# An eleven-place ring of expert weights kept up to expert 5, weight splits ordered behind the evictions, and two chunks of expert 1 requested during the last projection

## The reference

```python
h = layer_norm(x, ln0_g, ln0_b)
# mixer: proj = h @ w_in, cut into qkv, a, bt, z, xc, gb, gc, qm, gl (three gates)
qkv = silu(causal_depthwise_conv(qkv, conv_qkv)); q, k = l2_normalize(q), l2_normalize(k)
g = -(exp(a_log) * softplus(a + dt_bias)); beta = sigmoid(bt)
y_a = gated_rmsnorm(gated_delta_rule_chunked(q, k, v, g, beta)) * silu(z)
y_b = gb * causal_depthwise_conv(gc * xc, conv_mix)
y_m = softmax(qm @ km.T * 128 ** -0.5) @ vm          # km, vm = mem @ w_mem_kv
merged = sum(sigmoid(gl[b]) * (y[b] @ w_br[b]) for b in range(3))
h = layer_norm(ALPHA * h + merged @ w_o, ln1_g, ln1_b)
# experts: top 4 of 32 by h @ w_router + b_router, softmax over the four
for each expert e, for its tokens:
    gate, up = split(h @ w_gate_up[e] + b_gate_up[e])     # 1024 -> 2 x 1024
    hid = (clip(up, -7, 7) + 1) * (min(gate, 7) * sigmoid(1.702 * min(gate, 7)))
    ffn += weight * (hid @ w_down[e] + b_down[e])         # 1024 -> 1024
out = layer_norm(ALPHA * h + ffn, ln2_g, ln2_b)
```

## Times and profile before

| | us |
| --- | --- |
| median of 3 runs | 1283.3 |
| lowest, highest | 1281.4, 1283.37 |
| the profiled execution | 1282.62 |
| its span, first to last instruction | 1280.9 |
| TensorE busy in the span | 1217.3 (95%) |
| DMA moved | 453.62 MB, mean 354 GB/s |

### The profile page before, as it was taken

One profiled execution on the slowest core, in us unless ns is written; L12 is line 12 of the kernel. 1 busy time (PEld: TensorE's weight loads), 2 busy tenths in 40 slices (PEclk: granted clock), 3 DMA queues, 4 the chain that ended last, 5 costly groups with the idle time before them and its releaser, 6 DMA issues.

```text
span 1280.9 us, 16880 instructions
## 1 busy us (share of the span) xinstructions
PE 1217.3 (95%) x7135; PEld 616.2 (48%) x7135; DVE 392.6 (31%) x784; ACT 241.3 (19%) x387; POOL 146.1 (11%) x106
## 2 busy tenths in 40 slices
PE   6989999999999999999999999999999999999996
PEld 5789999998843333333333333333333333333332
DVE  5375553434521221221221221221112222122224
ACT  4355345444310000000000000000000000000001
POOL 8223432455200000000000000000000000000000
PEclk9899999999999999999999999999999999999998
DMA  9533323475799999999999999999999999999994
GB/s 299 200 133 132 115 85 128 171 304 196 277 401 420 398 427 426 420 431 428 430 435 428 431 430 427 433 431 427 430 430 430 432 432 426 429 432 430 426 425 179
DMA packets 49512, 453.62 MB, mean 354 GB/s; under 512 B 6110, under 2 KB 10283, under 8 KB 31019
## 3 DMA queue, kind: packets, MB, share of 16 engines
q1 hardware_dynamic: 49450, 452.71, 85.2%
HBM read 451.64 MB, written 1.05 MB: 353 GB/s over the span
## 4 chain that ended last, share of the span: by engine, by line
PE 72%; DMA 19%; DVE 3%; ACT 2%; POOL 2%; issue 1%; SPq 0%; ACTq 0%; DVEq 0%; POOLq 0%
PE bank L1386 27%; DMA late<-in_w_gate_up_dram 19%; PE bank L1459 13%; PE bank L1203 6%; PE bank L1204 5%; PE bank L1205 5%; PE bank L1472 4%; PE bank L1357 3%; PE bank L1372 2%; PE bank L1447 1%; ACT late L1175 1%; POOL w_lo L758 1%; ACT w_hi L1079 1%; PE bank L1467 1%; PE bank L559 1%
## 5 line engine op out<-in xcount | busy, mean ns | idle before, releaser
L1386 PE MATMUL bank<-late 128*64 128x512 f32 x1632 | 368.1, 598 | 10.4 <-DMA late<-in_w_gate_up_dram 10.2
L1386 PEld LDWEIGHTS bank<-late 128*64 128x64 f32 x1632 | 112.6, 137 | 242.2 <-issue 217.6
L1459 PE MATMUL bank<-late 128*64 128x512 f32 x816 | 182.5, 599 | 5.3 <-ACT late L1175 5.3
L1203 PE MATMUL bank<-act_hi,w_hi 128*128 128x256 f32 x448 | 130.1, 290 | 6.9 <-POOL w_lo L758 3.7
L1204 PE MATMUL bank<-act_lo,w_hi 128*128 128x256 f32 x448 | 126.5, 282 | 0.0
L1205 PE MATMUL bank<-act_hi,w_lo 128*128 128x256 f32 x448 | 126.4, 282 | 0.0
L1802 DVE TENSOR_SCALAR late<-bank 128x512 f32<-128x512 f32 x32 | 22.1, 692 | 306.2 <-PE bank L1386 306.1
L1459 PEld LDWEIGHTS bank<-late 128*64 128x64 f32 x816 | 56.9, 138 | 112.8 <-issue 104.4
L1386 PE MATMUL bank<-raw,late 128*64 128x512 f32 x416 | 93.4, 596 | 3.2 <-DMA raw<-in_w_gate_up_dram 3.2
L758 POOL TENSOR_TENSOR w_lo<-raw,w_hi 128x1024 fp32r<-128x1024 f32 x33 | 82.0, 2487 | 117.0 <-ACT w_hi L1079 116.9
L1203 PEld LDWEIGHTS bank<-act_hi,w_hi 128*128 128x128 f32 x448 | 85.1, 190 | 9.3 <-issue 4.1
(11 more groups left out here) (320 smaller groups left out, 1247.6 us busy)
## 6 DMA issues: line engine op xcount, KB each, us to landing
late<-in_w_gate_up_dram SPq DMA_DIRECT2D x38, 4096.0 KB, 31.8
late<-in_w_down_dram SPq DMA_DIRECT2D x51, 2048.0 KB, 30.6
late<-in_w_gate_up_dram SPq DMA_DIRECT2D x26, 2048.0 KB, 13.5
raw<-in_w_gate_up_dram SPq DMA_DIRECT2D x10, 4096.0 KB, 31.7
raw<-in_w_down_dram SPq DMA_DIRECT2D x13, 2048.0 KB, 32.9
raw<-in_w_in_dram SPq DMA_DIRECT2D x8, 2048.0 KB, 7.8
early<-in_w_in_dram SPq DMA_DIRECT2D x6, 2048.0 KB, 7.6
raw<-in_w_gate_up_dram SPq DMA_DIRECT2D x6, 2048.0 KB, 10.6
```

What stands on the lines that cost most here:

```text
L1203: mm(o, l_hi, r_hi, start=start, stop=False)
L1386: ins = mm(bk[64 * c:64 * c + 64, :], x_slotT[:, k % 4, 64 * (k // 4):64 * (k // 4) + 64], w[:, kk, at + 512 * c:at + 512 * (c + 1)], star ...
L1459: ins = mm(ps[3][64 * c:64 * c + 64, :], hidT[:, kk, 64 * q:64 * q + 64], w[:, kk, c * 512:(c + 1) * 512], start=(q == 0 and kk == 0), sto ...
```

## The change

Five things are done. In `mixer_schedule` the prep of a unit with one piece goes behind the unit, so on every engine its eviction comes ahead of the split; units with four pieces (`vm`, `wo`) stay as they are. SP requests chunks 6 and 7 (`second(0)`, `second(1)`) when the eight sums are done, between chunks 0 and 1; chunks 8 and 9 when `wo` is done; chunk 10 after `x1_added` and the one-hots. For this `src_hi` and `src_lo` change places in SBUF with `act_hi` and `act_lo`, and x1T moves into `once`. Chunks up to 32 (`WIDE_TO`) use eleven places in turn, m % 11; chunks 33 to 41 and then those from 42 count ten places from 0. The b_down loads follow chunk 41 (before: chunk 23).

```diff
-            out += [("prep", m + SPLITS) for m in uses[s] if m + SPLITS < 4 * N_MIX]
+            pieces = [("prep", m + SPLITS) for m in uses[s] if m + SPLITS < 4 * N_MIX]
             q += n
-        out.append(s)
+
+            out += pieces + [s] if n > 1 else [s] + pieces
+        else:
+            out.append(s)
...
+        src_hi, src_lo = (sb(n, [P, KD, T], F32R, early) for n in ("src_hi", "src_lo"))
         act_hi, act_lo = (sb(n, [P, KD, T], F32R, early) for n in ("act_hi", "act_lo"))
-        src_hi, src_lo = (sb(n, [P, KD, T], F32R, early) for n in ("src_hi", "src_lo"))
...
-        x1T = l.at(l.used - KD * T, KD, T)
...
+        x1T = l.at(once_o + 1024, KD, T)
...
+        PAIRED_FROM = (2 + ROUND) * EC
+        WIDE_TO = 3 * (RING + 1)
         LN2_SLOT = RAW
-        LAST_IN_LN2_SLOT = max(m for m in range(NE * EC) if m % RING == LN2_SLOT)
+        LAST_IN_LN2_SLOT = max(m for m in range(NE * EC) if (m - PAIRED_FROM) % RING == LN2_SLOT)
...
-            return m % RING if m < RING or m >= PAIRED_FROM else RING if m == RING else (m - 1) % RING
+            return m % (RING + 1) if m < WIDE_TO else (m - WIDE_TO) % RING if m < PAIRED_FROM else (m - PAIRED_FROM) % RING
...
+            def second(c):
+                chunk_dma(sp, c, w_gate_up[0, 1], w_down[0, 1], *ring_place(EC + c)[0:2])
+
             for c in range(RAW):
                 raw_spent(sp, N_MIX - RAW + (c - N_MIX) % RAW)
                 chunk_dma(sp, c, w_gate_up[0, 0], w_down[0, 0], *ring_place(c)[0:2])
+                if c == 0:
+
+                    wait_sums(sp, KD)
+                    second(0)
+                    second(1)
             sp.wait_ge(bank_full[bank_of(("wo", 1, 1))], turn_of(("wo", 1, 1)))
-            for c in range(EC):
-                if EC + c == RING - 1:
-
-                    sp.wait_ge(x1_added, 2 * NT)
-                if EC + c == RING:
-                    sp.wait_ge(onehots, 1)
-                if EC + c > RING:
-                    chunk_spent(sp, EC + c - RING - 1)
-                chunk_dma(sp, c, w_gate_up[0, 1], w_down[0, 1], *ring_place(EC + c)[0:2])
+            second(2)
+            second(3)
+            sp.wait_ge(x1_added, 2 * NT)
+            sp.wait_ge(onehots, 1)
+            second(4)
+            chunk_spent(sp, 0)
+            second(5)
             for ex in range(2, 2 + ROUND):
                 for c in range(EC):
                     m = EC * ex + c
-                    chunk_spent(sp, m - RING - (m <= 2 * RING))
+                    chunk_spent(sp, m - RING - 1)
                     chunk_dma(sp, c, w_gate_up[0, ex], w_down[0, ex], *ring_place(m)[0:2])
-                if ex == 3:
-                    chunk_spent(sp, RING)
+                if ex == 1 + ROUND:
+                    chunk_spent(sp, WIDE_TO - 1)
```

More of the change, by code:

```diff
@@ L833, in chunk_spent @@
                 eng.wait_ge(chunks_used, 4 * i + (c + 1 if c < 3 else 4))
-        PAIRED_FROM = (2 + ROUND) * EC
         EARLY_CHUNKS = {15: 3, 16: 4, 17: 5}
```

## The result

The changed kernel took **1286.8 us** (median of 20 runs, 1283.4 to 1289.4), the kernel before 1282.6 in the same comparison (20 runs, 1279.5 to 1286.0): a ratio of 1.0031, 95% interval 1.0022 to 1.0040. It is 4.2 us slower, above the range that was given. The profiled execution took 1289.2 us, 2.4 over its median, and its span is 1287.4.

The account below looks back on a forecast made before the run. The experts' weight stream was taken to bound the kernel, movable only before its queue is always full. 1282.6 - 1.2 (stream) + 0.3 (mixer: 2.7 - 1.6 - 0.8) = 1281.7 us, range 1279.0 to 1285.0.

Parts of the forecast that it names:

- The bound: From the first experts on: the end moves only with the weight stream, set by what happens before its queue is full.
- Both limits: Chunk 11's issue at 364.78 leaves 3.2 of 9.8 us head start; the pair 42 and 43, near 523, leaves 1.2.
- The first place: At the log decay, table load and SiLU now precede a split: +0.65 us at TensorE's wait, 0.1 of it carried on.
- The table load: ScalarE's activation table load in the mixer: costs about 1.28 us, without the further drain of about 1.38 us.
- limit at the pair: Chunks 42 and 43, issued near 523, can't land before 535.3: 1.2 us of gain remain and reach the end; bounds 0, 3.2.
- z2: Unit z 2 at the decay step: TensorE waits for GpSimd's w_lo near 105 and loses 2.7 us; bounds 0 and 3.4.
- returned waits: Mixer: four TensorE waits of about 0.4 us go, -1.6, and the sum's wait at 315.58 shortens, -0.8 us.
- one on the slow side: Rival 5: first place whole (3.4 us), nothing returned, b_down ahead of the pair eats the 1.2: 1286.0 us, chance 0.07.

Follow-up runs that it names:

- stream only: Changed kernel with the old order of splits ahead of evictions put back; early chunks, eleven places and moved b_down stay: 1282.4 us, ratio 1.0001.
- first place only: Changed kernel with split before eviction put back behind qkv 10 and qkv 11 alone; qkv 3 keeps the new order: 1280.8 us, ratio 0.9970.
- three back: Changed kernel with split before eviction put back behind qkv 3, qkv 10 and qkv 11: 1277.3 us, ratio 0.9960.
- 15 fillers: Changed kernel with 15 small unused matmuls in each of TensorE's two waits of 3.9 us: 1281.4 us, ratio 0.9986.
- without the overlap: Changed kernel, but VectorE starts its squares and subtraction of piece 23 only when GpSimd has ended piece 22: 1283.9 us, ratio 1.0015.

## Why the prediction was wrong

**Right.** The bound: every delay ahead of the stream reached the end (6.57 us at chunk 11's issue, 6.63 at the last DMA). Both limits: chunk 11 and the pair found an empty queue, and 3.2 us of head start were left behind chunk 11 (chunk 41 in stream only). Chunks 6 and 7 went out at once when the sums were done (324.45, that is 319.5 with TensorE's delay of 4.95 taken off). The first place: +0.65 foretold (1.7 for table load and SiLU, less 1.05), +0.70 measured (1.6 or 1.7 by first place only and the changed kernel against three back, less 1.02), and with a full clock 0.62 of it was given back on the way to z1, where I had put 0.55. The table load costs its 1.28 us and no more: the SiLU starts 1.29 us behind it (98.76, 100.05).

**Wrong, by the terms of the sum** (1282.6 - 1.2 + 0.3 = 1281.7):

| term | forecast | measured |
|---|---|---|
| stream, limit at the pair | -1.2 | +0.11 |
| z2, with the first place's 0.1 | +2.7 | +4.17 |
| behind the first wait, to z1 (the clock) | 0 | +1.25 |
| behind z2's wait, to lx0 (1.48 of it the clock) | 0 | +1.67 |
| returned waits | -2.4 | -3.63 |
| sum | -0.9 | +3.57 |

1. *The pair alone, and the step from it to the end.* "Alone, a pair would take 7.4 + 4.88 = 12.3" added the steady rate to a single chunk's landing. With an empty queue the pair took 13.3 us in the changed kernel and in stream only, 13.4 to 13.8 in five more kernels and 12.3 in one, that with 15 fillers:

```profile
520.09 0.37 SPq L803 DMA_DIRECT2D raw<-in_w_gate_up_dram  x1
```

```profile
raw<-in_w_gate_up_dram SPq DMA_DIRECT2D x1, 4096.0 KB, 12.3
```

So a single landing scatters by more than the 1.2 us that I took from one. And where the pair did land 1.1 us earlier behind expert 1 than before, in this last kernel, the next pair did not: 156.9 us behind expert 1's start, against 156.6 before, and the last DMA 831.89, against 832.01. "The 1.2 us reach the end" fails there as well. I had named 0 as the lower bound and took the row's difference instead, a small one between a measured number and one I had put together. The b_down loads stand right ahead of the pair in all eight; no run moves them away, so what they cost it is not separated.
2. *z2.* The chain was right, the duration of its last link was not: 2.39 us for GpSimd is the value with VectorE out of the way. The kernel before had the other value in its own trace, in the next instruction of GpSimd, beside VectorE's squares and a subtraction:

```profile
104.57 3.45 POOL L758 TENSOR_TENSOR w_lo<-raw,w_hi 128x1024 fp32r<-128x1024 f32 x1 [2.71 <-ACT w_hi L1079]
```

```profile
102.37 2.29 DVE L1669 TENSOR_TENSOR early<-early 128x2048 f32<-128x2048 f32 x1 [0.48 <-ACT early L1058]
104.58 1.22 DVE L758 TENSOR_TENSOR w_lo<-early,w_hi 128x1024 fp32r<-128x1024 f32 x1
```

From z1 to z2 I had 5.46 us, it took 6.93, and 5.77 in the run without the overlap: that settles 1.2 of the 1.5 us that were missing.
3. *The clock.* No term and no rival had it. A wait was priced at its length. The run with 15 fillers shows 1.25 and 1.48 us on top.
4. *Returned waits.* More came back than I had counted: from lx0 to the unit at 232.34 it is 1.98 us less (four waits of 0.4, not three), from there to the sum 1.65 less (the wait at 280.19, 0.79 of the sum's where I had put 0.8, and 0.45 in waits too short for the rows that I read). This term repeats to 0.1 us in every kernel with the new order. It was the only term that made the forecast too slow.

The rivals had one on the slow side: the first place whole, nothing returned, b_down eating the pair's 1.2. Its time (1286.0) is near the result, but its mechanism is refuted: 3.6 us were returned. The right total would have needed the price of an idle TensorE, which no rival had. What share of the medians' differences comes from the chance of an execution (two stretches with up to 3.9 us) stays open; the clock's part in them was seen, not controlled.

## What to carry to other kernels

Price a new wait of TensorE by its length plus what the granted clock loses behind it, and look in the trace for a matmul stretch behind a wait of the same size. Do not take a term of 1 us from one landing of a DMA: here the same transfer took 12.3 to 13.8 us on an empty queue. Before you take a duration of a GpSimd instruction with two operands from a row, see whether VectorE ran beside it there and whether it will in the new place. When a step is moved behind another, ask of each engine apart: here the eviction was free on VectorE, and the same order on ScalarE put a table load and a SiLU that waits for the eviction ahead of the split.

## What the runs showed of the hardware

**VectorE and GpSimd take turns.** A subtraction of two 128x1024 tiles on GpSimd takes 2.35 to 2.42 us alone. It took 3.51 us when it began 1.31 us before the end of VectorE's squares (2.29 us, undisturbed), and 3.45 when it began 0.09 us before the end of the squares with VectorE's next subtraction, 1.22 us, right behind them. VectorE's squares took 4.52 us when GpSimd's subtraction was ahead by 0.03 us, and its subtraction 3.37 instead of 1.22 us. The one that comes second pays; the first does not. The Trainium skill (SBUF — State Buffer, 🔬 SBUF: two separate sides) says so: the shared port pair is an exclusive lock, taken for the whole instruction by whichever starts first, also for a VectorE operation with two inputs in SBUF against a GpSimd operation that reads SBUF. By that rule z2 would wait 1.3 us more than my sum had, the time left of the squares; the trace shows 1.1 to 1.2.

**An idle TensorE can cost more than its wait.** The waits of 3.8 to 3.9 us, six in four executions without fillers, all had a granted clock of 0.66 to 0.88 in the stretch of 10 us at or behind their end, a mean over time at 1.2 and at 2.4 GHz; filled, in two executions, it was 1.00 each time. Behind waits of 2.2 us at the log decay it was 0.83 in four executions and 1.00 in one, behind waits of 1.9 us 1.00 in three. The length of the wait alone does not decide it: behind z2's wait of 2.68 us in the kernel without the overlap the clock was 1.00. 15 unused matmuls of 128x128 in each wait made the changed kernel 5.4 us faster, from 0.3% slower than before to 0.14% faster.

**A pair on an empty queue.** 2 MB (chunks 0 and 11) landed 7.2 to 7.8 us after the issue, 4 MB (the first pair, eight kernels) after 12.3 to 13.8, in most of them later than the 7.4 + 4.88 = 12.3 of the sum.
